# A decoder layer on one core: re-laid first and last stages, decays in pieces, both heads of a tile taken together

## The reference

```python
mod = silu(c) @ w_ada + b_ada                       # sh1, sc1, gt1, sh2, sc2, gt2; shf, scf from w_ada_final
h   = rmsnorm(x, norm1_g) * (1 + sc1) + sh1
# mixer: 4 GLA heads (dk 64, dv 128) and 4 HGRN2 heads (dk = dv = 128) on slices of h @ w_in, chunkwise:
#   S_t = diag(exp(log_g_t)) S_{t-1} + k_t^T v_t ;  o_t = q_t S_t, then head rmsnorm and silu gate
x   = x + gt1 * (concat(heads) @ w_out)
h2  = rmsnorm(x, norm2_g) * (1 + sc2) + sh2
x   = x + gt2 * moe(h2)                             # top group of 4, top 2 of its 8 experts, SwiGLU, 256 wide
out = rmsnorm(x, norm_f_g) * (1 + scf) + shf
```

## Time and profile before

| | us |
|---|---|
| median of 3 runs | 1254.56 |
| their range | 1249.68 to 1256.32 |
| the profiled execution, its own time | 1251.96 |
| its span in the trace | 1250.1 |
| TensorE busy in the span | 1094.2 (88%) |
| VectorE busy | 638.3 (51%) |
| ScalarE busy | 322.5 (26%) |

### The profile page before, as it was taken

How to read it: one execution, slowest core, us unless ns; L and a number is a source line. 1 busy time by engine, 2 the same in 40 slices (tenths; PEclk the granted TensorE clock), 3 DMA queues, 4 the chain that set the end, 5 groups by cost and what they waited for, 6 DMA issues and landing times.

```text
span 1250.1 us, 16745 instructions
## 1 busy us (share of the span) xinstructions
PE 1094.2 (88%) x6524; PEld 854.7 (68%) x6524; DVE 638.3 (51%) x1384; ACT 322.5 (26%) x619; POOL 147.4 (12%) x289
## 2 busy tenths in 40 slices
PE   1789999999999999998699996099999999999964
PEld 1568788878897888887544442087887788778621
DVE  8735366826794959686433244533233233323237
ACT  2435422542265455445211111000000000000121
POOL 0200010000100000000000002322222222221100
PEclk9989979999999999999799998589999999999977
DMA  9400231223323242322751215348888888886055
GB/s 362 147 18 17 68 101 52 85 85 85 95 75 119 68 136 85 102 85 95 267 218 67 68 51 206 81 155 317 341 311 317 315 339 316 305 333 259 27 220 191
DMA packets 85112, 205.74 MB, mean 165 GB/s; under 512 B 17254, under 2 KB 45990, under 8 KB 76860
## 3 DMA queue, kind: packets, MB, share of 16 engines
q1 hardware_dynamic: 63328, 156.79, 34.8%
q0 software_dynamic: 15248, 42.65, 10.8%
q10 hardware_dynamic: 6476, 5.47, 1.4%
HBM read 188.57 MB, written 24.71 MB: 171 GB/s over the span
## 4 chain that ended last, share of the span: by engine, by line
PE 75%; DVE 10%; DMA 6%; ACT 5%; issue 2%; POOL 1%; ACTq 0%; SPq 0%; POOLq 0%; DVEq 0%
PE PS L1842 18%; PE PS L1796 9%; PE PS L1849 9%; PE PS L1640 8%; PE PS L1642 8%; PE PS L1641 8%; PE PS L1701 4%; DMA WOUT<-in_w_out 3%; PE PS L1834 2%; PE PS L1901 2%; DVE ACC L1104 1%; PE PS L1806 1%; PE PS L1721 1%; PE PS L1719 1%; PE PS L1707 1%
## 5 line engine op out<-in xcount | busy, mean ns | idle before, releaser
L1842 PE MATMUL PS<-XGT,WGU 128*128 128x96 f32 x2048 | 236.3, 277 | 0.0
L1842 PEld LDWEIGHTS PS<-XGT,WGU 128*128 128x128 f32 x2048 | 234.8, 194 | 0.5 <-issue 0.5
L1640 PE MATMUL PS<-WH,HT 128*128 128x256 f32 x512 | 151.1, 295 | 4.7 <-ACT GVB L880 2.0
L1641 PE MATMUL PS<-WL,HT 128*128 128x256 f32 x512 | 148.2, 290 | 0.0
L1642 PE MATMUL PS<-WH,HL 128*128 128x256 f32 x512 | 148.1, 289 | 0.0
L1267 DVE COPY_PREDICATED AT<-MASK,PS 128x64 f32<-128x64 uint8 x320 | 72.9, 228 | 98.7 <-PE PS L1707 75.9
L1796 PE MATMUL PS<-WOUT,OT 128*128 128x512 f32 x256 | 114.6, 607 | 7.5 <-DMA WOUT<-in_w_out 4.2
L1849 PE MATMUL PS<-WDN,ATT 128*96 128x512 f32 x256 | 115.0, 592 | 0.0
L1050 ACT ACTIVATE SIL<-PS 128x192 f32<-128x192 f32 x32 | 10.6, 331 | 380.5 <-PE PS L1842 380.5
L1640 PEld LDWEIGHTS PS<-WH,HT 128*128 128x128 f32 x512 | 101.8, 199 | 9.1 <-issue 8.6
L1641 PEld LDWEIGHTS PS<-WL,HT 128*128 128x128 f32 x512 | 102.1, 199 | 0.0
(11 more groups left out here) (279 smaller groups left out, 1568.6 us busy)
## 6 DMA issues: line engine op xcount, KB each, us to landing
WGU<-in_w_exp_gate SPq DMA_DIRECT2D x32, 1024.0 KB
WGU<-in_w_exp_up SPq DMA_DIRECT2D x32, 1024.0 KB
WDN<-in_w_exp_down SPq DMA_DIRECT2D x32, 1024.0 KB
AR<-in_w_ada POOLq DMA_DIRECT2D x32, 512.0 KB, 3.8
WF<-in_w_in SPq DMA_DIRECT2D x28, 512.0 KB, 4.9
AST<-in_w_ada SPq DMA_DIRECT2D x16, 512.0 KB, 9.1
AR<-in_w_ada_final POOLq DMA_DIRECT2D x16, 512.0 KB, 3.8
YG<-expert_rows SPq DMA_DIRECT2D x8, 1024.0 KB, 6.8
```

What stands on the lines that cost most here:

```text
L1640: MM(ps, wh, xh, start=first, stop=False)
L1641: MM(ps, wh, xl, start=False, stop=False)
L1842: last = MM(GU[par][:, col:col + C], WGU[slot][:, m, k, j * P:(j + 1) * P], XGT[:, par, k, :], start=(k == 0), stop=(k == KD - 1))
```

## The change

- **First stage.** The x transposes use PSUM banks of their own (`X_BANK`, tiles `XB`), the two columns others (`COL`). Six blocks of the first half are transposed ahead of the columns, two more within the first product; two products without use stand between the columns. ScalarE scales the first four tiles of x. The low part takes one pass from PSUM and one from SBUF. Six blocks of the second half stand behind the product k, two behind `ga`, and the squares of its tiles come after the first half on ScalarE. The loads of GpSimd start when 12 slices have been used.
- **Decays.** `decay` becomes `decay_steps`: add, clamp, and the scan in two halves, one piece behind a step (behind each second step in GLA units). Slices and low parts have other steps.
- **GLA units.** `paired_levels` issues the 64-row products of both heads of a tile in turn, in `LV[0]` and `LV[1]`. The state's product and the output's second product take all 128 rows, the state `S` having one tensor a head whose other 64 rows are zero.
- **Unit 5 and `w_out`.** The row is taken at step 4. The `WOUT` loads don't wait for each other.
- **Last stage.** All eight `YG` loads at once in eight buffers, three PSUM buffers, four `OUTT`. For tiles 4 to 7 TensorE adds the residual too (`SUM_ON_PE = 4`), and squares and scaling read PSUM. The inverse root takes three operations, with a factor -2 that `GSF` makes good (`HALVED`). 13 products without use stand ahead of the sums.

```diff
-    ROW_STEP = {0: 12, 1: 8}
-    SLICE_STEPS = {0: [0, 1, 2, 3, 4, 5, 6, 7, 12, 13, 14, 15], 1: [0, 1, 2, 3, 8, 9, 10, 11, 12, 13, 14, 15],
-                   2: range(5), 3: range(5), 4: range(5), 5: []}
-    SLICES_BETWEEN = 3
+    ROW_STEP = {0: 12, 1: 8, UNITS - 1: 4}
+    SLICE_STEPS = {0: [1, 3, 5, 5, 9, 9, 11, 11, 13, 13, 15, 15], 1: [1, 3, 3, 5, 9, 9, 11, 11, 13, 13, 15, 15],
+                   2: [0, 1, 6, 7], 3: [0, 1, 6, 7], 4: [0, 1, 6, 7], 5: []}
+    SLICES_BETWEEN = 4
+    X_BANK = [2, 3, 4, 5, 6, 1, 2, 3, 4, 5, 6, 7, 2, 3, 4, 5]
+    X_AHEAD = 6
...
-        S = at("S", 203.25, [P, 2, P])
+        S = [at("SA", 203.25, [P, 2, P]), at("SB", 199, [P, 2, P])]
...
-            for n in range(2):
-                load_chunk(n)
+            load_chunk(0)
             for g in range(2, NT // 2):
                 load_x(g)
-            for n in range(2, WSLOTS):
+            for n in range(1, WSLOTS):
                 load_chunk(n)
...
             for v in range(8):
-                if v >= 1:
-                    sp.wait_ge(wout_in, 16 * v)
                 sp.dma_start(WOUT[:, v, :], wo_rows[:, v, :]).then_inc(wout_in, 16)
...
-            for t in range(4):
-                load_rows(t)
             for t in range(NT):
-                if t + 4 < NT:
-                    sp.wait_ge(ysum_ready, t + 1)
-                    load_rows(t + 4)
+                sp.dma_start(YG[t][:, :, :], ys_rows[:, 0:3:2, t, :]).then_inc(yg_in[t], 16)
+            for t in range(NT):
                 sp.wait_ge(out_ready, t + 1)
...
-            pool.wait_ge(x_in[NT // 2 - 1], 16)
+            pool.wait_ge(ast_used, KD + 4)
...
             root_of(0, 4, D).then_inc(rr_ready, 1)
+            act.wait_ge(inv_ready, 1)
+            for t in range(4):
+                A(XR[:, t, :], XR[:, t, :], ACT.Copy, scale=RR[:, t:t + 1]).then_inc(xr_ready, 1)
...
-                    n = number[("xT", g, k)]
-                    v_.wait_ge(xh_ready, g * KD + k + 1)
-                    V.tensor_scalar(HFULL[:, k, hs], PJ[n % 2], GS1[:, k:k + 1], SH1[:, k:k + 1],
-                                    ALU.mult, ALU.add).then_inc(pj_free[n % 2], 1)
-                    v_.wait_ge(pj_free[n % 2], n // 2 + 1)
-                    V.tensor_tensor(HL[:, k, hs], HFULL[:, k, hs], HT[:, k, hs].bitcast(F32), ALU.subtract).then_inc(xl_ready, 1)
-
+                    i = g * KD + k
+                    v_.wait_ge(xh_ready, i + 1)
+                    V.scalar_tensor_tensor(out=HFULL[:, k, hs], in0=XB[i], scalar=GS1[:, k:k + 1],
+                                           in1=HT[:, k, hs].bitcast(F32), op0=ALU.mult,
+                                           op1=ALU.subtract).then_inc(xt_done, 1)
+                    v_.wait_ge(xt_done, i + 1)
+                    V.tensor_scalar(HL[:, k, hs], HFULL[:, k, hs], SH1[:, k:k + 1], None, ALU.add).then_inc(xl_ready, 1)
...
+                first = [add, clamp] if is_gla(u) else [arrived]
+                return first + [lambda: scan(0), lambda: scan(1)]
...
                     attention_step(n)
                     m = n - first_step[u]
-                    if m == 2 and u + 1 < UNITS:
-                        decay(u + 1)
-                    if m in SLICE_STEPS[u]:
+                    at_m = (m - 3) // 2 if is_gla(u) else m - 2
+                    if 0 <= at_m < len(later) and (m % 2 or not is_gla(u)):
+                        later[at_m]()
+                    for _ in range(list(SLICE_STEPS[u]).count(m)):
                         unit_slice()
-                    if u + 1 < UNITS and m == (11 if is_gla(u) else 3):
-                        lows(u + 1, v_chunks(u + 1))
+                    if u + 1 < UNITS and m in ((7,) if is_gla(u) else (4, 5)):
+                        for j in range(2) if is_gla(u) else (m - 4,):
+                            low(u + 1, v_chunks(u + 1)[j][0])
...
+            def minus_twice_inverse(t):
+                r, m = RR[:, t:t + 1], TA[:, t:t + 1]
+                link(V.reciprocal(r, r))
+                link(V.scalar_tensor_tensor(out=m, in0=m, scalar=r, in1=r, op0=ALU.mult, op1=ALU.mult))
+                return V.scalar_tensor_tensor(out=r, in0=m, scalar=-3.0, in1=r, op0=ALU.add, op1=ALU.mult)
...
+            pe.wait_ge(ios, 5)
+            x_transposes(0, range(X_AHEAD))
+            col_job("sc1", ACC, ast_used, KD)
+            for _ in range(2):
+                MM(PJ[0], IDENT[:], XR[:, 0, 0:HALF], start=True, stop=True)
+            col_job("sh1", ACCB, ast_used, 2 * KD)
...
+                        if half == 0 and k == 2:
+                            x_transposes(0, range(X_AHEAD, KD))
...
+            def state_product(n):
+                u, t, h = steps[n]
+                return MM(LV[n % 2][:, (NL + 1) * P:(NL + 2) * P], KH[:, t, :], values(u, t, h), start=True, stop=True)
+
+            def paired_levels(u, t):
+                n, ts = first_step[u] + 2 * t, slice(t * P, (t + 1) * P)
+                if n > 0:
+                    pe.wait_ge(at_ready, n)
+                for l in range(NL):
+                    for h in range(2):
+                        rows = slice(64 * h, 64 * h + 64)
+                        MM(LV[h][:, l * P:(l + 1) * P], XL[rows, l, ts], XL[rows, l, ts], start=True, stop=True)
...
-                    last = MM(OP[n % 2], QE[rows, t * P:(t + 1) * P], S[rows, t % 2, :], start=False, stop=True)
+                    last = MM(OP[n % 2], QE[:, t * P:(t + 1) * P], S[h][:, t % 2, :], start=False, stop=True)
...
+                if is_gla(u):
+                    for t in range(NT):
+                        n = lo + 2 * t
+                        paired_levels(u, t)
+                        for h in range(2):
+                            if t > 0:
+                                output(n + h - 2)
+                            if t < NT - 1:
+                                state_product(n + h).then_inc(lv_ready, 1)
+                        if 2 * t == ROW_STEP[u]:
+                            row_job(UNIT_ADA[u], ar_used, KD * (u + 1))
+                        last = gv_half(u, NT // 2 + t // 2, t % 2)
...
+            for _ in range(13):
+                MM(SQ[:, 0:HALF], IDENT[:], GSF[:, 0:HALF], start=True, stop=True)
             pe.wait_ge(diag_ready, 1)
             for t in range(NT):
-                pe.wait_ge(yg_in[t % 4], 16 * (t // 4 + 1))
-                if t >= 2:
-                    pe.wait_ge(x2_ready, t - 1)
+                pe.wait_ge(yg_in[t], 16)
+                if t >= 3 + SUM_ON_PE:
+                    pe.wait_ge(out_scaled, t - 2)
+                elif t >= 3:
+                    pe.wait_ge(x2_ready, t - 2)
                 for half in range(2):
                     hs = slice(half * HALF, (half + 1) * HALF)
+                    if t >= SUM_ON_PE:
+                        MM(YS[t % 3][:, half, :], IDENT[:], X1[:, t, hs], start=True, stop=False)
```

249 lines of the change are left out of this document (135 added, 114 removed).

## The result

The changed kernel takes **1188.44 us** (median of 4 runs, 1186.56 to 1190.16) against 1254.19 in the same comparison (4 runs, 1249.68 to 1256.32): ratio 0.948, 95% interval 0.945 to 0.951. The forecast was 1195 with a range of 1184 to 1214. The profiled execution took 1190.16 us for a span of 1188.3, against 1251.96 and 1250.1.

What follows compares the result with a forecast made beforehand. TensorE, busy 88% of the span, was taken as the bound until VectorE comes to the front. Terms -15.5 - 15.5 - 11.5 - 5 - 1.5 - 10.5 = -59.5 on 1251.96 gave 1192.5, with the median's 2.6 1195 us; range 1184 to 1214.

Steps and rivals of the forecast that it cites:

- First stage: Start up to unit 0: earlier first product and no waits behind it, up to 17.7 us possible, -15.5 taken.
- The fear of half pace behind the transposes of the second half: First stage: if the clock falls again behind the six blocks (3.6 us), the gain is 14 us.
- Units 0 and 1: GLA units: paired 64-row products and fewer row changes make a tile 6.0 us; -15.5 and -11.5 us.
- The step on which the chances hung: GLA units: weight loads of both halves overlap, so twelve 64-row products take 1.35 us, not 2.7; little better than even.
- The cold start that I had added to unit 0: Unit 0's beginning: slow first levels as before, ten records in 2.29 us instead of 1.28, added to 54.5 us.
- HGRN2 units: Units 2 to 4: decay in halves behind steps 3 and 4 removes TensorE's wait, 3 x -1.7 = -5 us.
- Unit 5 and `WOUT`: Unit 5 to output projection: 4.17 us wait for weights goes, fourth slice delays the first step; -1.5, between -4 and +4.
- Last stage: Behind the last expert: sums at full clock, tiles 4 to 7 with six products; -10.5 us, between -6 and -13.
- products in turn: Rival, GLA units: 64-row products of both heads run in turn, each unit about 6.5 us longer; 1208, chance 0.30.
- The ends: Rival, first stage, unit 5 and last stage: they give less back, 3 + 2 + 4 us; 1204, chance 0.13.
- VectorE steps of 2.2 us: Rival, GLA units: a step with signals takes 2.2 instead of 1.85, giving 16 us, not 27; 1206, chance 0.06.
- One sign of being wrong: GLA units: TensorE waiting for VectorE in most tiles was listed as showing the forecast wrong.
- A price for a change between halves: Rival, GLA levels: each change between halves costs as much as a change of rows; 1275 at 0.2 us, chance 0.05.

Runs made afterwards that it cites:

- e12_first_stage: Changed kernel with VectorE scaling the first four tiles again and the low part reading PSUM, then subtracting again: 1195.2 us, ratio 0.9552.
- e6_late_transposes: Changed kernel with the six block transposes put behind both columns again: 1189.98 us, ratio 0.9511.
- e1_in_turn: Changed kernel with the same 64-row products, but one head's five levels after the other's: 1199.36 us, ratio 0.9609.
- e8_u5_slices: Changed kernel with two of the four slices ahead of unit 5 moved behind its steps 1 and 2: 1179.31 us, ratio 0.9424.
- e9_all_slices: On top of e8_u5_slices, slices of the GLA units moved to where VectorE stands idle: 1174.44 us, ratio 0.9393.
- e4_decay_whole: Changed kernel with both half scans behind step 2 in the HGRN2 units, slices left where the change put them: 1190.12 us, ratio 0.9522.
- e7_wout_waits: Changed kernel with the loads of the output weights waiting for each other again: 1189.63 us, ratio 0.9493.
- e11_u5_wout_waits: e8_u5_slices with the loads of the output weights waiting for each other again, as in e7_wout_waits: 1185.11 us, ratio 0.9487.

## Why the prediction was right, and where not

The result lies in the range, 6.6 us under the point. Of these 2.3 are in the sum (1192.5 forecast, 1190.16 profiled), 4.3 in the 2.6 carried over from the median: this time the profiled run was 1.7 above its median, not 2.6 below.

- **First stage**, -15.5 forecast, -19.4 measured, beyond the 17.7 called possible (by the other starts of unit 0, 132.3 to 135.7 us, it is -17.5 to -20.9). The first product was placed right (38.26 for 38.3), the q of the second half 1.6 us early (68.6 for 70.2). The fear of half pace behind the transposes of the second half was not borne out: six blocks took 2.7 us, not 3.6, and everything behind ran at full pace. That VectorE is the path is shown by `e12_first_stage`. That transposes ahead of the sums help is not (`e6_late_transposes`).
- **Units 0 and 1**, -27 forecast, -33.3 measured. The step on which the chances hung, weight loads of both halves overlapping, is right, shown by order alone (`e1_in_turn`), and in full: 12 records alone take 1.53 us and 24 in pairs 1.54, at 0.064 a record, where half of 0.112 is 0.056 and the changes between 64 and 128 rows come on top. The Trainium skill (TensorEngine Tiling (Array Packing), Key Properties) says that different tiles can run weight loads and matmuls in parallel. By these two figures the trace agrees. A tile with one slice took 6.2 to 6.4 us for the 6.0 forecast; against 6.37, two slices cost 0.3 (6.67 in unit 1) where 0.4 was forecast, and a half scan with two slices 1.3 (7.68 in unit 0) where 1.6 was. The cold start that I had added to unit 0 (first levels at the lower clock) didn't come in this profile, but came in the ten others with these pairs: at 56.4 us unit 0 has 2.9 us less than the 59.3 forecast (54.5 and 4.8 for the cold start), and 4.4 less in this profile.
- **Between the units** the forecast had 0, measured +5.3 (+0.9 and +2.7 in `e8_u5_slices`). This is the step that failed outright: I costed the slices behind the last steps inside the tiles and did not ask who waits behind the unit. The factors of the next unit start behind 2.6 us of slices, ScalarE's work with them, and TensorE then waits and runs at the lower clock; without those slices both waits are shorter (`e9_all_slices`). The units gave 6.3 us more than forecast and the stretches behind them took 5.3 back; with the other terms off by 1.2 to 4.3 us either way, the sum came within 2.3 us of the trace. That it came so close is luck.
- **HGRN2 units**, -5 forecast, -7.2 measured, for the wrong reason. The wait was read rightly and is gone, but I gave the gain to the decay in pieces, which is worth 0 (`e4_decay_whole`). That the slice behind the same step had caused the wait is the likely reading, not a shown one.
- **Unit 5 and `WOUT`**, -1.5 forecast, +2.8 measured, inside -4 to +4. The mechanism was named, but the size was wrong: "the fourth is loaded 1.3 us later" took the distance between the issues for that between the landings, which is 4.9 us, so that the first copy came 4.9 us later where one to four were forecast. The blame on 15 other loads is refuted (`e7_wout_waits`: 0.3 us). The wait for `WOUT` went as forecast and was worth nothing until unit 5 was mended (`e11_u5_wout_waits`).
- **Last stage**, -10.5 forecast, -11.7 measured: first sum 11.4 us behind the last expert (11.5 by the prediction's 1196, 12.5 by the 1197 that its sum goes by), last sum 34.4 us after the first (35.5, or 34.5 from 1197). The products without use give 2.8 of it, the split of the adds 2.9. Some 6 us no run isolates; the prediction didn't name the second wait for the expert rows, 4.14 us at 1220.23, which went with the loads at once.
- The stretch that nothing touches is 1.7 us longer (564.7). In `e8_u5_slices` and `e9_all_slices` it takes 563.0 and 563.3, so that is no effect of the change.

Of the rivals, products in turn cost 11 us (`e1_in_turn`), where 13 were forecast, but with part of the overlap left; what they cost without any, no run shows alone. The ends gave more, not less, and no tile had VectorE steps of 2.2 us (two took 3.75). One sign of being wrong did come: TensorE waited for VectorE ahead of 12 of the 16 tiles, 9.0 us in all. The prediction's own tile, 6.0 us against 5.7 of TensorE's work, implies such waits, so that sign was badly chosen. A price for a change between halves is excluded by the 0.064 us a record. A change between 64 and 128 rows costs 0.1 to 0.2 us.

## What to carry to other kernels

When small transfers stand in a queue of their own with two buffers, count the distance between landings, not between issues, and put their consumers where the engine is idle, not between the last step of a stage and the factors of the next. Cost every stage together with the wait behind it: time saved ahead of a wait for another engine is not saved, and a gain can lie hidden behind a new delay until that is mended (0 against 5.8 us for the same edit). Products on half the rows belong in pairs, alternating between the halves.

## What the hardware showed that I had not expected

- Pairing float32 products of 64 rows with 128 weight columns gives the whole factor of two, weight loads included: 12 records in 1.53 us, 24 in 1.54. And a product on one half starts ahead of earlier ones on the other half (156.83 against 156.94 and 157.05).
- Full-width products do not always lift the pace: four records of them took 3.76 us between the columns (0.94 each, where the same shape took 0.44 at the end) and left the next column at 3.96 us, and the first product at 0.43 a pass where 0.23 is full pace. Thirteen at the end, behind a busy stretch, held it (granted clock 1.00 from 1134.4 to 1145.8).
- At the start of the program the granted clock did not tell the pace: these four records took 3.76 us at 0.50 in the changed kernel (26.4 to 30.2) and at 1.00 in `e6_late_transposes` (25.6 to 29.3).
- The clock differs between kernels with the same program up to there: unit 0's first levels took 1.4 us once and 2.1 to 2.5 in the ten other profiles with these pairs. A pause of 2.04 us behind unit 0 left the next product at full pace (11.7 us, granted clock 1.00), one of 3.25 us was followed by 6 us at 0.50 (14.4). But one of 3.26 us (`e8_u5_slices`) was followed by only 3.7 us near 0.50 (13.2), and one of 2.24 us (`e9_all_slices`) by 3.4 us of it (13.2), so the length of the pause alone does not decide.
